# Stick-breaking attention: the product of keep factors taken by a scan before a transpose, or as a sum of logarithms by triangular matmuls

## The reference

```
z = (q @ k.T) * d**-0.5                    # scores, (512, 512) per head
mask = s < t                               # key position s before query position t
log_keep = where(mask, log_sigmoid(-z), 0)
suffix = reverse_cumsum(log_keep) - log_keep     # over s, exclusive
a = where(mask, exp(log_sigmoid(z) + suffix), 0)
o = a @ v
```

## Time and profile before

| | before |
|---|---|
| median of 3 runs | 1693.63 us (1693.46 to 1696.76) |
| the profiled execution | 1693.63 us, of it span 1691.8 us |
| TensorE matmul (PE) busy | 1663.6 us, 98% |
| TensorE weight load (PEld) busy | 1376.4 us, 81% |
| VectorE (DVE) busy | 924.6 us, 55% |
| ScalarE (ACT) busy | 613.1 us, 36% |
| GpSimd (POOL) busy | 120.7 us, 7% |
| DMA | 91 GB/s mean |
| mean granted TensorE clock | 0.996 |

### The profile page before, as it was taken

How to read it: one execution, slowest core, us unless ns; L and a number is a source line. 1 busy time by engine, 2 the same in 40 slices (tenths; PEclk the granted TensorE clock), 3 DMA queues, 4 the chain that set the end, 5 groups by cost and what they waited for, 6 DMA issues and landing times.

```text
span 1691.8 us, 20713 instructions
## 1 busy us (share of the span) xinstructions
PE 1663.6 (98%) x7550; PEld 1376.4 (81%) x7550; DVE 924.6 (55%) x1077; ACT 613.1 (36%) x695; POOL 120.7 (7%) x107
## 2 busy tenths in 40 slices
PE   7999999999999999999999999999999999999996
PEld 5888888888888888888788888888888888888885
DVE  6357754466575556633252486545656665655233
ACT  4233333322345454522133323343223544454121
POOL 7000000000130000002100000000003100000021
PEclk9999999999999999999999999999999999999998
DMA  4222213112322222222232222122122222223221
GB/s 171 100 87 75 73 65 107 68 63 88 100 100 91 96 99 99 94 92 100 83 108 98 88 75 75 66 96 72 66 100 90 98 99 96 91 98 100 100 92 71
DMA packets 42487, 153.45 MB, mean 91 GB/s; under 512 B 4784, under 2 KB 4912, under 8 KB 42160
## 3 DMA queue, kind: packets, MB, share of 16 engines
q1 hardware_dynamic: 40896, 146.82, 25.3%
q10 hardware_dynamic: 864, 3.54, 0.7%
q0 software_dynamic: 656, 2.10, 0.3%
HBM read 150.34 MB, written 2.10 MB: 90 GB/s over the span
## 4 chain that ended last, share of the span: by engine, by line
PE 98%; DVE 1%; DMA 0%; issue 0%; POOL 0%; ACT 0%; DVEq 0%; SPq 0%; POOLq 0%
PE ps L703 30%; PE ps L705 30%; PE ps L704 30%; PE ps L794 2%; PE ps L752 2%; PE ps L778 2%; PE ps L767 1%; PE ps L786 1%; PE ps L876 0%; DMA w_raw<-wts 0%; PE ps L756 0%; DVE gate L693 0%; DVE rinv L690 0%; POOL ssum L320 0%; DVE w_lo L472 0%
## 5 line engine op out<-in xcount | busy, mean ns | idle before, releaser
L703 PE MATMUL ps<-u_hi,w_hi 128*128 128x512 f32 x1344 | 530.8, 395 | 0.0
L705 PE MATMUL ps<-u_hi,w_lo 128*128 128x512 f32 x1344 | 523.7, 390 | 0.0
L704 PE MATMUL ps<-u_lo,w_hi 128*128 128x512 f32 x1344 | 523.0, 389 | 0.0
L472 DVE TENSOR_TENSOR w_lo<-w_raw,w_hi 128x1024 fp32r<-128x1024 f32 x276 | 355.8, 1299 | 291.1 <-ACT w_hi L337 285.2
L337 ACT ACTIVATE w_hi<-w_raw 128x1024 fp32r<-128x1024 f32 x276 | 287.6, 1056 | 297.3 <-DMA w_raw<-wts 297.0
L705 PEld LDWEIGHTS ps<-u_hi,w_lo 128*128 128x128 f32 x1344 | 252.3, 188 | 53.4
L704 PEld LDWEIGHTS ps<-u_lo,w_hi 128*128 128x128 f32 x1344 | 252.5, 188 | 52.5 <-issue 0.5
L703 PEld LDWEIGHTS ps<-u_hi,w_hi 128*128 128x128 f32 x1344 | 252.4, 188 | 51.9 <-issue 0.5
L703 PE MATMUL ps<-g_hi,w_hi 128*128 128x512 f32 x352 | 136.9, 389 | 0.0
L704 PE MATMUL ps<-g_lo,w_hi 128*128 128x512 f32 x352 | 136.9, 389 | 0.0
L705 PE MATMUL ps<-g_hi,w_lo 128*128 128x512 f32 x352 | 136.9, 389 | 0.0
(11 more groups left out here) (138 smaller groups left out, 1947.4 us busy)
## 6 DMA issues: line engine op xcount, KB each, us to landing
w_raw<-wts SPq DMA_DIRECT2D x276, 512.0 KB, 3.2
dec<-decay ACTq DMA_DIRECT2D x2, 1024.0 KB, 5.8
out<-gate SPq DMA_DIRECT2D x6, 256.0 KB, 2.9
x<-xt POOLq DMA_DIRECT2D x5, 256.0 KB, 7.2
cs<-rope ACTq DMA_DIRECT2D x2, 512.0 KB, 4.0
x<-xt SPq DMA_DIRECT2D x2, 256.0 KB, 3.8
out<-gate POOLq DMA_DIRECT2D x2, 256.0 KB, 3.0
x<-xt ACTq DMA_DIRECT2D x1, 256.0 KB, 5.4
```

The lines of the kernel that those rows point to most:

```text
L472: nc.vector.tensor_tensor(w_lo[:, s, :], w_raw[:, s, :], w_hi[:, s, :].bitcast(F32), ALU.subtract).then_inc(s_lo, 1)
L703: nc.tensor.matmul(dst, a_hi, b_hi, start=start, stop=False)
L704: nc.tensor.matmul(dst, a_hi, b_lo, start=False, stop=False)
L705: return nc.tensor.matmul(dst, a_lo, b_hi, start=False, stop=stop)
```

## The change

The suffix product is taken as a sum of logarithms on TensorE. The scores are computed with keys on the partitions from the start (stationary and moving operand swapped, same widths). ScalarE takes |z|, exp(-|z|) and ln(1 + that); VectorE adds max(z, 0), which gives sp(z) in `att`; ScalarE and VectorE split it into `sp_hi` and `sp_lo`. `suffix` then multiplies both parts by a triangular matrix of -1 (`tri`) and by a matrix of -1 (`neg1`), and adds the products onto z in PSUM. ScalarE takes exp of the result, and both parts of that are made as before for `weigh`, which is unchanged. There is no transpose, no scan and no `mark`. The step takes the place of `turn` behind slab 19+3h (`TRI_AT`).

```diff
-TURN_AT = {19 + 3 * h: h for h in range(SB_HEADS)}
+TRI_AT = {19 + 3 * h: h for h in range(SB_HEADS)}
@@ gpsimd, start
-            nc.gpsimd.tensor_copy(negb[:], gate[:, 0, 0:P]).then_inc(s_cc, 1)
+            nc.gpsimd.tensor_copy(tri[:], gate[:, 0, 0:P]).then_inc(s_cc, 1)
+            nc.gpsimd.tensor_scalar(neg1[:], onesf, -1.0, None, ALU.mult).then_inc(s_cc, 1)
+            nc.gpsimd.tensor_copy(negb[:], gate[:, 0, P:2 * P]).then_inc(s_cc, 1)
             nc.gpsimd.tensor_copy(idb[:], idf).then_inc(s_cc, 1)
-            nc.gpsimd.memset(mark[:], 0).then_inc(s_cc, 1)
-            pool.wait_ge(s_cc, 3)
-            for c in range(TT):
-                nc.gpsimd.memset(mark[:, BLK[c] + WIDTH[c] - 1:BLK[c] + WIDTH[c]], 1).then_inc(s_cc, 1)
@@ scalar, behind slab 19+3h
-                        act.wait_ge(s_turn, l * 8 + h + 1)
-                        nc.scalar.activation(sp_hi[:], psf[:, E0:E0 + ECOLS], ACT.Copy).then_inc(s_ah, 1)
+                        act.wait_ge(s_tri, l * 8 + h + 1)
+                        nc.scalar.activation(att[:], psf[:, E0:E0 + ECOLS], ACT.Exp).then_inc(s_a, 1)
+                        act.wait_ge(s_a, l * 8 + h + 1)
+                        nc.scalar.activation(sp_hi[:], att[:], ACT.Copy).then_inc(s_ah, 1)
@@ scalar, behind slab 17+3h
-                        nc.scalar.activation(att[:], psf[:, E0:E0 + ECOLS], ACT.Sigmoid, scale=-1.0).then_inc(s_keep, 1)
-                        nc.scalar.activation(beta[:], psf[:, E0:E0 + ECOLS], ACT.Sigmoid).then_inc(s_beta, 1)
+                        nc.scalar.activation(att[:], psf[:, E0:E0 + ECOLS], ACT.Abs).then_inc(s_abs, 1)
+                        act.wait_ge(s_abs, l * 8 + h + 1)
+                        nc.scalar.activation(att[:], att[:], ACT.Exp, scale=-1.0).then_inc(s_ln, 1)
+                        act.wait_ge(s_ln, l * 16 + 2 * h + 1)
+                        nc.scalar.activation(att[:], att[:], ACT.Ln, bias=1.0).then_inc(s_ln, 1)
...
+                        act.wait_ge(s_sp, l * 8 + QK_AT[i] + 1)
+                        nc.scalar.activation(sp_hi[:], att[:], ACT.Copy).then_inc(s_sph, 1)
@@ vector, behind slab 19+3h
-                        nc.vector.tensor_tensor(sp_lo[:], psf[:, E0:E0 + ECOLS], sp_hi[:].bitcast(F32), ALU.subtract).then_inc(s_al, 1)
+                        nc.vector.tensor_tensor(sp_lo[:], att[:], sp_hi[:].bitcast(F32), ALU.subtract).then_inc(s_al, 1)
@@ vector, behind slab 17+3h
-                        nc.vector.tensor_tensor_scan(att[:, ::-1], att[:, ::-1], mark[:, ::-1], 1.0,
-                                                     ALU.mult, ALU.max).then_inc(s_scan, 1)
...
-                        nc.vector.tensor_tensor(beta[:, 0:ECOLS - 1], beta[:, 0:ECOLS - 1], att[:, 1:ECOLS],
-                                                ALU.mult).then_inc(s_a, 1)
+                        dve.wait_ge(s_ln, l * 16 + 2 * h + 2)
+                        nc.vector.scalar_tensor_tensor(out=att[:], in0=psf[:, E0:E0 + ECOLS], scalar=0.0, in1=att[:],
+                                                       op0=ALU.max, op1=ALU.add).then_inc(s_sp, 1)
+                        dve.wait_ge(s_sph, l * 8 + h + 1)
+                        nc.vector.tensor_tensor(sp_lo[:], att[:], sp_hi[:].bitcast(F32), ALU.subtract).then_inc(s_spl, 1)
@@ tensor
-            def turn(l, h):
-
-                pe.wait_ge(s_a, l * 8 + h + 1)
+            def suffix(l, h):
+
+                pe.wait_ge(s_spl, l * 8 + h + 1)
                 for c in (0, 1, 3, 2):
-                    for t in range(c, TT):
-                        o = E0 + BLK[c] + (t - c) * P
-                        a = BLK[TT - 1 - t] + c * P
-                        mm = nc.tensor.transpose(psf[:, o:o + P], beta[:, a:a + P], idf)
-                mm.then_inc(s_turn, 1)
+                    for part in (sp_hi, sp_lo):
+                        for c2 in range(c, TT):
+                            o = E0 + BLK[c] + (c2 - c) * P
+                            mm = nc.tensor.matmul(psf[:, o:o + WIDTH[c2]], tri[:] if c2 == c else neg1[:],
+                                                  part[:, BLK[c2]:BLK[c2] + WIDTH[c2]], start=False, stop=True,
+                                                  skip_group_check=True)
+                mm.then_inc(s_tri, 1)
```

More of the change, by code:

```diff
@@ L111, in sb @@
                 n *= s
-            size = n * {BF16: 2, mybir.dt.uint8: 1}.get(dt, 4)
+            size = n * (2 if dt == BF16 else 4)
             if where is None:
@@ L131, in trunk @@
         epsf = cst[:, 2, TT:TT + 1]
-        mark = sb("mark", [P, ECOLS], mybir.dt.uint8)
+        tri = sb("tri", [P, P], F32R)
+        neg1 = sb("neg1", [P, P], F32R)
         idb = sb("idb", [P, P], BF16)
@@ L165, in trunk @@
         att = sb("att", [P, ECOLS], F32, TMP)
-        beta = sb("beta", [P, ECOLS], F32, G_ + 16 * K)
         ynorm = sb("ynorm", [P, TT, 256], F32, TMP + 5 * K)
@@ L208, in trunk @@
         s_qk = sem("s_qk")
-        s_keep = sem("s_keep")
-        s_beta = sem("s_beta")
-        s_scan = sem("s_scan")
+        s_abs = sem("s_abs")
+        s_ln = sem("s_ln")
+        s_sp = sem("s_sp")
+        s_sph = sem("s_sph")
+        s_spl = sem("s_spl")
+        s_tri = sem("s_tri")
         s_a = sem("s_a")
-        s_turn = sem("s_turn")
         s_pv = sem("s_pv")
@@ L295, in _ @@
             pool.dma_start(cst[:], consts[:, 0:3, :]).then_inc(s_cst, 16)
-            pool.dma_start(gate[:, 0, 0:P], consts[:, 3, :]).then_inc(s_cst, 16)
+            pool.dma_start(gate[:, 0, 0:2 * P].rearrange("p (a b) -> p a b", a=2), consts[:, 3:5, :]).then_inc(s_cst, 16)
             pool.wait_ge(s_par, 16)
@@ L389, in _ @@
                             nc.scalar.activation(dst, src, ACT.Copy, scale=rcol[:, tt:tt + 1]).then_inc(s_vt, 1)
-                    if i in TURN_AT:
-                        h = TURN_AT[i]
-                        act.wait_ge(s_turn, l * 8 + h + 1)
-                        nc.scalar.activation(sp_hi[:], psf[:, E0:E0 + ECOLS], ACT.Copy).then_inc(s_ah, 1)
+                    if i in TRI_AT:
+                        h = TRI_AT[i]
+                        act.wait_ge(s_tri, l * 8 + h + 1)
+                        nc.scalar.activation(att[:], psf[:, E0:E0 + ECOLS], ACT.Exp).then_inc(s_a, 1)
+                        act.wait_ge(s_a, l * 8 + h + 1)
+                        nc.scalar.activation(sp_hi[:], att[:], ACT.Copy).then_inc(s_ah, 1)
                     if i in PV_AT:
@@ L434, in _ @@
                                                  bias=pcol(l, PAR_BG + k)).then_inc(s_gate, 1)
+                    if i in QK_AT:
+                        act.wait_ge(s_sp, l * 8 + QK_AT[i] + 1)
+                        nc.scalar.activation(sp_hi[:], att[:], ACT.Copy).then_inc(s_sph, 1)
                     split_hi(l, i + AHEAD)
@@ L523, in _ @@
                                                            op1=ALU.subtract).then_inc(s_vl, 1)
-                    if i in TURN_AT:
-                        dve.wait_ge(s_ah, l * 8 + TURN_AT[i] + 1)
-                        nc.vector.tensor_tensor(sp_lo[:], psf[:, E0:E0 + ECOLS], sp_hi[:].bitcast(F32), ALU.subtract).then_inc(s_al, 1)
+                    if i in TRI_AT:
+                        dve.wait_ge(s_ah, l * 8 + TRI_AT[i] + 1)
+                        nc.vector.tensor_tensor(sp_lo[:], att[:], sp_hi[:].bitcast(F32), ALU.subtract).then_inc(s_al, 1)
                     if i in PV_AT:
@@ L630, in _ @@
                         h = QK_AT[i]
-                        if h == 0:
-                            dve.wait_ge(s_cc, 3 + TT)
-                        dve.wait_ge(s_keep, l * 8 + h + 1)
-                        nc.vector.tensor_tensor_scan(att[:, ::-1], att[:, ::-1], mark[:, ::-1], 1.0,
-                                                     ALU.mult, ALU.max).then_inc(s_scan, 1)
-                        dve.wait_ge(s_beta, l * 8 + h + 1)
-                        dve.wait_ge(s_scan, l * 8 + h + 1)
-                        nc.vector.tensor_tensor(beta[:, 0:ECOLS - 1], beta[:, 0:ECOLS - 1], att[:, 1:ECOLS],
-                                                ALU.mult).then_inc(s_a, 1)
+                        dve.wait_ge(s_ln, l * 16 + 2 * h + 2)
[3 more added lines that the diff above has]
+                        nc.vector.tensor_tensor(sp_lo[:], att[:], sp_hi[:].bitcast(F32), ALU.subtract).then_inc(s_spl, 1)
                     split_lo(l, i + AHEAD)
@@ L749, in scores @@
                 for c in (0, 1, 3, 2):
[L750 to L753, removed]
+                    for n, (k_part, q_part) in enumerate(((k_hi, q_hi), (k_hi, q_lo), (k_lo, q_hi))):
+                        nc.tensor.matmul(psf[:, E0 + BLK[c]:E0 + BLK[c] + WIDTH[c]], k_part[:, c * P:(c + 1) * P],
+                                         q_part[:, c * P:S], start=(c != 3 and n == 0), stop=False, skip_group_check=True)
                 for c in (0, 1, 3, 2):
-                    o = E0 + BLK[c] + WIDTH[c]
-                    mm = nc.tensor.matmul(psf[:, o - P:o], idb[:], negb[:], start=False, stop=(c != 1),
```

(23 more changed lines are left out.)

## The result

| | before | after |
|---|---|---|
| median | 1694.25 us (1693.46 to 1696.76, 4 runs) | 1722.27 us (1721.60 to 1723.91, 4 runs) |
| ratio, 95% interval | | 1.0165 (1.0152 to 1.0177) |
| span of the profiled execution | 1691.8 us | 1721.6 us |
| forecast | | 1719.5 us (1714.5 to 1728.0) |

The change costs 28.0 us, 1.65%; 25.9 were forecast. First the page's busy times and chain of the changed kernel, which answer to the earlier trace rows.

The account below looks back on a forecast made before the run. TensorE's own stream was taken to bound the kernel: 25.8 us for the longer stream, 0.5 for waits and -0.4 at the start gave 25.9 on 1693.63, thus 1719.5 us, range 1714.5 to 1728 us.

Parts of the forecast that it names:

- The bound: Whole run: TensorE, busy 1663.6 of 1691.8 us, sets the time; in the attention each microsecond added to its stream adds one.
- Transposes: TensorE, each head: the ten transposes that go give back 1.01 us, about 0.10 each.
- The suffix: TensorE, each head: twenty new matmuls take 2.62 us, 1.61 more net of transposes, 25.8 us over 16 heads.
- upper bound: Highest cost of the twenty matmuls: 0.11 for each 128 but the last, 2.96 us a head, 31.2 us net in all.
- Same weight, loaded again: TensorE's new matmuls: a stationary operand equal to the one ahead is loaded again, so `neg1` saves nothing.
- The first wait: Sums for `suffix`: ready at 9.47 us, TensorE asks at 10.78, no wait; 0 to 0.2 at each layer's first head.
- The second wait: Weights for `weigh`, heads 1 and 3: second `sp_lo` ends at 18.69 us, TensorE asks at 18.97, 0.3 to spare.
- TensorE's question: How much longer TensorE's own stream gets in the attention: 1.61 us for each head, 25.8 us over 16 heads.
- Start: Start of the run: GpSimd loses the write of `mark`, its sums end earlier, TensorE's weight load gains at most 0.4 us.
- Rival A: ScalarE: a table switch holds it twice its record, sums and weights come late, 10 us more, 1730 us; chance 7%.
- Rival B: Hand-overs between engines cost 0.2 us each, `sp_lo` late at heads 1 and 3, 5 us more, 1725 us; chance 12%.
- Rival C: Not slower: `suffix` streams in the transposes' 1.01 us plus small allowances, time at most 1697 us; chance 2%.

Follow-up runs that it names:

- e4_transposes: The changed kernel with the twenty `suffix` matmuls replaced by the ten transposes of before, the new ScalarE and VectorE chain kept: 1701.97 us against 1696.54, ratio 1.0035.
- e1_hi_only: The changed kernel with `suffix` taken of the high part alone, ten matmuls, low part left out: 1704.70 us against 1696.54 for the kernel before, ratio 1.0043.
- e9_mask_on_vector: The kernel before with each head's four mask matmuls taken off TensorE and done by eight VectorE operations: 1692.21 us against 1694.94, ratio 0.9981.
- e5_slab_earlier: The changed kernel with `suffix` one slab earlier, behind slab 18+3h: 1835.98 us against 1694.94 for the kernel before, ratio 1.0834.
- e7_vector_delay: The changed kernel with two unused VectorE operations added ahead of each head's second `sp_lo`: 1740.40 us against 1694.94 for the kernel before, ratio 1.0266.

## Why the prediction was right, point by point

- **The bound.** Right: TensorE is busy through the whole attention of both kernels, and 27.3 of the 28.0 us lie in its two stretches.
- **Transposes.** 1.01 us for each head, as read; the periods differ by 1.70 with it.
- **The suffix.** 2.62 forecast, 2.71 measured; the 1.4 us over 16 heads are two thirds of what the forecast fell short. The reading of a lone 128 as 0.06 was wrong in form: the 128 takes 0.06 (154.46 to 154.52), but the matmul behind it is later by about as much. The 512 behind a 128 takes 152.67 - 152.39 = 0.28 instead of 0.23, the 384 behind one 0.23 instead of 0.177. Five such followers add about 0.25 that the sum did not have. Against that, the last 128 has no gap behind it, 0.06 where 0.20 was booked. It is luck that the second error took back half of the first. That a 128 costs 0.11 was in the upper bound, and should have been the value: 1.90 for the others, seven times 0.11 and 0.06 for the last make 2.73.
- **Same weight, loaded again.** Right: 160 more loads for 160 more matmuls.
- **The first wait.** Right: ready at 9.47 forecast, 9.49 measured, 1.3 to spare. Two small errors cancel in it: an activation of ScalarE starts 0.03 behind the one that it needs (142.29 behind 141.02 + 1.24), not 0.10, and one that reads `att` takes 1.28, not 1.24. At the first heads 0.3 us of a weight load, and the head's period is 0.10 to 0.15 longer: inside 0 to 0.2.
- **The second wait.** Right: 18.69 against 18.70 (159.72 - 141.02), 0.3 to spare against 0.35. What the prediction did not say is that this room was made by the suffix itself; `e4_transposes` and `e1_hi_only` missed their numbers for that reason, and I should have seen it, since the 1.61 stood in the sum for TensorE's question.
- **Start.** -0.4 was forecast. The profiled start came 1.4 later, not earlier, in a part that moves by over 3 us between runs. The weight load's wait of 0.4 for GpSimd's sums is no longer listed, but it is not listed in `e9_mask_on_vector` either, which still writes `mark`. It stays open whether the 0.4 was gained. By the medians, 28.0 less the 27.3 of the attention leaves 0.7 where -0.4 was booked, which is the other part of what the forecast fell short.
- **Rival A** (a table switch holds ScalarE twice as long) is refuted by the rows: the load at 143.58 ends at 144.86 and Ln starts at 144.88, though Ln needs the result of the Exp ahead of it. The same holds at all 16 loads ahead of Ln: 1.29 to 1.30 us from the load's start to that of Ln. The Trainium skill (ScalarE: Activation LUTs, What ACT_TABLE_LOAD costs) has a drain of about 1380 ns beside each load. No such time stands here. **Rival B** is refuted by the 0.35 us left at head 1 and by the list of waits, which has none for `sp_lo` at heads 1 and 3. **Rival C** fails at 2.71 us for what had to fit in about 1.2.

## What to carry to other kernels

Where one engine is busy throughout, price a change by the distances between starts in its stream, and check for each other engine only whether its result is there when the busy engine asks. Work moved from an idle engine onto the busy one is paid in full (1.70 us for each head here), while 105 us added to ScalarE cost next to nothing, as long as the results were there in time. Room found in a chain may be made by the very work that is to be cut: compute it again with the shorter stream before promising the gain.

## What had not been expected of the hardware

- A wait of TensorE can cost more than its length. Behind waits of 4.0 us the suffix ran at the lower clock and took 5.18 us instead of 2.71 (`e5_slab_earlier`). Behind a gap of 2.2 us the clock was at the lower level for about 10 us in two of four places, which cost 4.6 us each, and stayed at 1.00 in the other two (`e7_vector_delay`). Behind the gaps of 1.6 us in `e4_transposes` the matmuls kept their distance of 0.23. Where between these the fall sets in was not tried.
- The first matmul behind a wait costs 0.11 us more than the wait: 156.78 to 157.12 is 0.34 for 512 columns instead of 0.23. It is not the wait alone that does this: the first score matmul of each head takes 0.34 too, where no wait is listed (157.12 to 157.46 before the change).
- A block of 128 columns costs about 0.11 us in every order of the widths tried, part of it in the start of the matmul behind it, though it streams in about half of that (an estimate: a quarter of the 0.227 of 512 columns).
